# Two more places for expert weight pieces in an expert-choice MoE layer on one Trainium2 core

## What is computed

```python
def ec_moe(x, router_w, w1, w3, w2):
    probs = softmax(xf @ router_w)
    gates, idx = top_k(probs.T, cap)            # cap = 2 * N // 16: 64 and 16 rows
    xe = xf[idx]
    h = silu(xe @ w1) * (xe @ w3)               # per expert 1024 x 2048, twice
    ye = (h @ w2) * gates                       # per expert 2048 x 1024
    out = zeros_like(xf).at[idx].add(ye)

x = x + gate1 * (concat([o, s]) @ w_out)
h2 = rmsnorm(x, norm2_w) * (1 + scale2) + shift2
x = x + gate2 * ec_moe(h2, router_w, w1, w3, w2)
y = rmsnorm(x, final_norm_w)
```

## Time and profile before

| | |
|---|---|
| time, median of 3 runs (lowest, highest) | 1450.53 us (1450.44, 1455.31) |
| the profiled execution: its own time, its span | 1455.17 us, 1453.3 us |
| PE busy, share of the span | 1391.0 us, 96% |
| DVE, ACT, POOL busy | 356.9, 163.7, 56.0 us |
| HBM read, written | 455.67 MB, 13.37 MB |
| the loop of experts 1 to 14 | 489.3 to 1368.9 us |

### The profile page before, as it was taken

The page is one execution under the profiler, slowest core; times in us unless marked ns, Lnnn a source line. Parts: engine busy times, 40 slices in busy tenths (PEclk is TensorE's granted clock), DMA queues, the critical chain, the costliest instruction groups (busy, mean ns, idle before and its releaser), DMA issues.

```text
span 1453.3 us, 24452 instructions
## 1 busy us (share of the span) xinstructions
PE 1391.0 (96%) x10960; PEld 511.1 (35%) x10960; DVE 356.9 (25%) x709; ACT 163.7 (11%) x263; POOL 56.0 (4%) x65
## 2 busy tenths in 40 slices
PE   5899999899879999999999999999999999999994
PEld 2354544755533232323333333332323333232321
DVE  3116153523632111303111130211203111130314
ACT  3263324111120000000000000000000000000011
POOL 0200000000000000000000000000000000000000
PEclk8999999799989999999999999999999999999997
DMA  9433313401656999999999999999999999999995
GB/s 358 160 118 115 107 51 109 154 30 58 263 222 279 396 409 413 411 417 400 426 402 412 414 412 417 401 412 414 410 417 402 425 399 412 414 410 417 414 411 213
DMA packets 73357, 469.56 MB, mean 323 GB/s; under 512 B 4749, under 2 KB 6626, under 8 KB 32362
## 3 DMA queue, kind: packets, MB, share of 16 engines
q1 hardware_dynamic: 67200, 451.36, 76.3%
q0 software_dynamic: 5200, 17.17, 4.2%
q10 hardware_dynamic: 922, 0.52, 0.1%
HBM read 455.67 MB, written 13.37 MB: 323 GB/s over the span
## 4 chain that ended last, share of the span: by engine, by line
PE 85%; DMA 11%; DVE 2%; issue 1%; SPq 1%; ACT 1%; POOLq 0%; ACTq 0%; POOL 0%; DVEq 0%
PE psum L1016 41%; PE psum L1032 12%; PE psum L663 9%; DMA ring<-in_exp_w_dram 9%; PE psum L1043 6%; PE psum L876 5%; PE psum L707 2%; PE psum L644 1%; DMA ring<-in_ada_w_dram 1%; PE psum L967 1%; PE psum L901 1%; PE psum L850 1%; SPq L546 1%; PE psum L854 1%; DMA both<-xn_dram,both 1%
## 5 line engine op out<-in xcount | busy, mean ns | idle before, releaser
L1016 PE MATMUL psum<-ring,both 128*32 128x512 f32 x6144 | 665.4, 593 | 1.9 <-DMA ring<-in_exp_w_dram 0.8
L1016 PEld LDWEIGHTS psum<-ring,both 128*32 128x32 f32 x6144 | 198.0, 110 | 462.7 <-issue 434.7
L1032 PE MATMUL psum<-ring,both 128*32 128x512 f32 x2048 | 233.6, 597 | 6.3 <-DMA ring<-in_exp_w_dram 5.8
L1745 DVE TENSOR_TENSOR both<-both,psum 128x512 f32<-128x512 f32 x48 | 49.5, 1032 | 555.4 <-PE psum L1016 555.4
L663 PE MATMUL psum<-ring,feat 128*128 128x512 f32 x320 | 138.3, 593 | 0.0
L1321 ACT ACTIVATE both<-psum 128x512 f32<-128x512 f32 x48 | 28.7, 597 | 952.1 <-PE psum L1016 887.1
L1032 PEld LDWEIGHTS psum<-ring,both 128*32 128x32 f32 x2048 | 65.2, 110 | 154.0 <-issue 143.8
L1043 PE MATMUL psum<-ring,both 128*32 128x512 f32 x1024 | 118.7, 592 | 0.0
L663 PEld LDWEIGHTS psum<-ring,feat 128*128 128x128 f32 x320 | 60.5, 190 | 76.4 <-issue 76.3
L1763 DVE SCALAR_TENSOR_TENSOR both<-psum,both 64x512 f32<-64x512 f32 x32 | 24.0, 749 | 224.2 <-PE psum L1043 224.0
L876 PE MATMUL psum<-ring,both 128*128 128x512 f32 x160 | 73.9, 618 | 0.0
(11 more groups left out here) (221 smaller groups left out, 604.6 us busy)
## 6 DMA issues: line engine op xcount, KB each, us to landing
ring<-in_exp_w_dram SPq DMA_DIRECT2D x192, 2048.0 KB, 25.0
ring<-in_ada_w_dram SPq DMA_DIRECT2D x12, 2048.0 KB, 12.5
ring<-in_w_in_dram SPq DMA_DIRECT2D x4, 2048.0 KB, 12.8
ring<-in_w_out_dram SPq DMA_DIRECT2D x2, 2048.0 KB, 10.6
acc_dram<-x POOLq DMA_DIRECT2D x5, 512.0 KB, 2.9
xn_dram<-feat POOLq DMA_DIRECT2D x5, 512.0 KB, 2.9
x<-acc_dram SPq DMA_DIRECT2D x5, 512.0 KB, 26.5
out_dram<-feat SPq DMA_DIRECT2D x5, 512.0 KB, 10.4
```

What stands on the lines that cost most here:

```text
L1016: mm = nc.tensor.matmul(role_bank(role)[f4 * PART:(f4 + 1) * PART, :], xe[:, kt, part * PART:(part + 1) * PART], w[:, kt % 2, f4 * 512:(f4 ...
L1032: mm = nc.tensor.matmul(role_bank("Y_A")[at:at + PART, :], h[:, c, part * PART:(part + 1) * PART], w[:, f, half * 512:(half + 1) * 512], s ...
L1745: role_stored(nc.vector.tensor_tensor(h_rows[:, part, :].rearrange("p (c a) -> p a c", a=PART), silu_h[:, part % 2, :].rearrange("p (a c) ...
```

## The change

The four sample tiles of x, and those in `feat`, are each just the size of a piece. Both buffers become places for expert pieces: `IN_X` and `IN_FEAT`, so there are eight. Pieces are counted through all experts (n = 12 x expert + m) and go to place `EXPERT_SLOT[n % 8]`. Twelve isn't a multiple of eight, but 24 is, so the loops of SP and PE now take two experts in a body, and `piece_place` gives place and count for both; the loops of ACT and DVE stay as they are. A piece is loaded when the piece eight before it has been read.

Pieces 0 and 1 of expert 0 go to the new places and are the first that SP issues: piece 0 when the four sample tiles of x are saved and normed, piece 1 when the normed rows are saved and PE has turned them. The wait for the attention's last output comes then, ahead of piece 2. The load of the gate piece now stands ahead of piece 5 and behind pieces 0 to 4. At the end, the loads of x move from ahead of piece 9 to behind piece 11 and wait until PE has read piece 5 of the last expert. POOL waits for the saves of x ahead of its first gather.

```diff
-EXPERT_SLOT = [3, 4, 5, 2, 0, 1]
-LOADS_BEFORE = [CHUNK_SLOT.count(s) for s in range(RING)]
+IN_X, IN_FEAT = RING, RING + 1
+EXPERT_SLOT = [IN_X, IN_FEAT, 3, 4, 5, 2, 0, 1]
+PIECES = len(EXPERT_SLOT)
+LOADS_BEFORE = [CHUNK_SLOT.count(s) for s in range(PIECES)]
 EXPERT_LOADS = 12
+
+
+def piece_place(m, expert, ahead):
+
+    odd = not isinstance(expert, int)
+    n = EXPERT_LOADS * ((1 if odd else expert) + ahead) + m
+    slot = EXPERT_SLOT[n % PIECES]
+    loads = 16 * (LOADS_BEFORE[slot] + n // PIECES + 1)
+    per_expert = 16 * EXPERT_LOADS // PIECES
+    return slot, loads - per_expert + expert * per_expert if odd else loads
+
...
-        x = sb("x", TILES * D)[:].rearrange("p (t d) -> p t d", t=TILES)
+        x_all = sb("x", TILES * D)
...
         def chunk(slot):
+            if slot == IN_X:
+                return x_all[:, 0:CHUNK_F]
+            if slot == IN_FEAT:
+                return feat[:, 0:CHUNK_F]
             return ring[:, slot * CHUNK_F:(slot + 1) * CHUNK_F]
...
-        def wait_expert_chunk(pe, m, expert):
-            slot = EXPERT_SLOT[m % RING]
-            pe.wait_ge(slot_loaded[slot], 16 * (LOADS_BEFORE[slot] + m // RING + 1) + expert * (16 * EXPERT_LOADS // RING))
+        def wait_expert_chunk(pe, m, expert, ahead):
+            slot, loads = piece_place(m, expert, ahead)
+            pe.wait_ge(slot_loaded[slot], loads)
             return chunk(slot)
...
-        def wait_expert_chunk_read(sp, m, expert):
+        def wait_expert_chunk_read(sp, m, expert, ahead):
 
             back, m = (1, m + EXPERT_LOADS) if m < 0 else (0, m)
-            when = expert - back
+            when = expert + (ahead - back) if ahead != back else expert
...
-            def load_expert_chunk(m, expert):
-                slot = EXPERT_SLOT[m % RING]
+            def load_expert_chunk(m, expert, ahead=0):
+                slot, loads = piece_place(m, expert, ahead)
+                expert = expert + ahead if ahead else expert
...
 
 
-            wait_filled(sp, JOB["o", TILES - 1])
-            sp.wait_ge(o_ready, TILES)
-            for m in range(RING):
-                if m == 3:
+            for m in range(PIECES):
+                slot = EXPERT_SLOT[m]
+                if slot == IN_X:
+                    sp.wait_ge(acc_saved, 16 * ST)
+                    sp.wait_ge(xn2_ready, ST)
+                elif slot == IN_FEAT:
+                    sp.wait_ge(xn2_saved, 16 * ST)
+                    wait_filled(sp, JOB["hT", ST - 1, 0])
+                    wait_filled(sp, JOB["hT", ST - 1, 1])
+                elif slot == 3:
+                    wait_filled(sp, JOB["o", TILES - 1])
+                    sp.wait_ge(o_ready, TILES)
+                elif slot == 2:
                     wait_trunk_chunk_read(sp, CHUNK_OF["out", 0])
                     sp.dma_start(chunk(CHUNK_SLOT[CHUNK_OF[ADA[11]]]).rearrange("p (k n) -> p k n", k=KT), ada_k[:, :, 5632:6144])\
                         .then_inc(slot_loaded[CHUNK_SLOT[CHUNK_OF[ADA[11]]]], 16)
-                if m >= 3:
-                    wait_trunk_chunk_read(sp, chunk_before(EXPERT_SLOT[m], len(TRUNK_CHUNKS)))
+                if slot < TRUNK_RING:
+                    wait_trunk_chunk_read(sp, chunk_before(slot, len(TRUNK_CHUNKS)))
                 load_expert_chunk(m, 0)
-            for m in range(RING, EXPERT_LOADS):
-                wait_expert_chunk_read(sp, m - RING, 0)
+            for m in range(PIECES, EXPERT_LOADS):
+                wait_expert_chunk_read(sp, m - PIECES, 0, 0)
                 load_expert_chunk(m, 0)
-            with sp.Fori(1, LAST) as expert:
-                for m in range(EXPERT_LOADS):
-                    wait_expert_chunk_read(sp, m - RING, expert)
-                    load_expert_chunk(m, expert)
+            with sp.Fori(1, LAST, 2) as expert:
+                for ahead in range(2):
+                    for m in range(EXPERT_LOADS):
+                        wait_expert_chunk_read(sp, m - PIECES, expert, ahead)
+                        load_expert_chunk(m, expert, ahead)
             for m in range(EXPERT_LOADS):
-                if m == 9:
-                    sp.wait_ge(acc_saved, 16 * (TILES + LAST))
-                    for t in OUT_ORDER:
-                        sp.dma_start(x[:, t, :], acc_dram[t * P:(t + 1) * P, :]).then_inc(acc_loaded[t], 16)
-                wait_expert_chunk_read(sp, m - RING, LAST)
+                wait_expert_chunk_read(sp, m - PIECES, LAST, 0)
                 load_expert_chunk(m, LAST)
+            sp.wait_ge(w13_read, 6 * EXPERTS)
+            sp.wait_ge(acc_saved, 16 * (TILES + LAST))
+            for t in OUT_ORDER:
+                sp.dma_start(x[:, t, :], acc_dram[t * P:(t + 1) * P, :]).then_inc(acc_loaded[t], 16)
...
             pool.wait_ge(xn2_saved, 16 * ST)
+            pool.wait_ge(acc_saved, 16 * ST)
...
-            def expert_products(expert, first=False, last=False):
+            def expert_products(base, ahead=0, first=False, last=False):
+                expert = base + ahead if ahead else base
...
             expert_products(0, first=True)
-            with pe.Fori(1, LAST) as expert:
-                expert_products(expert)
+            with pe.Fori(1, LAST, 2) as expert:
+                for ahead in range(2):
+                    expert_products(expert, ahead)
```

More of the change, by code:

```diff
@@ L208, in trunk_kernel @@
         router_amp = sb("router_amp", 2 * KT * EXPERTS)[:].rearrange("p (w k e) -> p w k e", w=2, e=EXPERTS)
-        x = sb("x", TILES * D)[:].rearrange("p (t d) -> p t d", t=TILES)
+        x_all = sb("x", TILES * D)
+        x = x_all[:].rearrange("p (t d) -> p t d", t=TILES)
         feat = sb("feat", TILES * D)
@@ L292, in trunk_kernel @@
         psum_stored = [sem(f"psum_stored{b}") for b in range(BANKS)]
-        slot_loaded = [sem(f"slot_loaded{s}") for s in range(RING)]
+        slot_loaded = [sem(f"slot_loaded{s}") for s in range(PIECES)]
         extra_loaded = {name: sem(f"extra_loaded_{name}") for name in EXTRA}
@@ L1022, in up_chunk @@
                 def up_chunk(which, k2):
-                    return wait_expert_chunk(pe, EXPERT_CHUNKS.index((which, k2)), expert).rearrange("p (k n) -> p k n", k=2)
+                    return wait_expert_chunk(pe, EXPERT_CHUNKS.index((which, k2)), base, ahead).rearrange("p (k n) -> p k n", k=2)
                 def down_sample(i, w):
@@ L1047, in down_chunk @@
                 def down_chunk(i):
-                    return wait_expert_chunk(pe, 8 + i, expert).rearrange("p (k n) -> p k n", k=4)
+                    return wait_expert_chunk(pe, 8 + i, base, ahead).rearrange("p (k n) -> p k n", k=4)
                 if first:
```

## The result

The changed kernel takes 1515.95 us in the median of four runs (1510.72 to 1518.85), the kernel before 1450.49 beside it: ratio 1.0446, 95% interval 1.0414 to 1.0477. Forecast were 1449.7 us and a range up to 1470.5, so the time lies 66 us above the forecast and 45 above the range. It is rival B's direction: B had 19.6 us more than before, measured are 65.5. The profiled execution took 1510.72 us, its span 1508.9.

A forecast was written before the change was run, and what follows sets the result against it. PE and weight transfers were taken as level in the loop, the end as hanging on transfers. Gate weights 4.5 us later, stalls gone, jumps covered: x's scaling sets the end, 1450.5 - 0.8 = 1449.7 us, range 1444.5 to 1470.5.

The forecast's parts named there:

- rival B: PE's loop: body not held, each jump back stops PE for two packets; 25.8 us in all, 1470.1 us; chance 0.32.
- Part 4: PE's loop body of two experts: jumps back cost 0 to 3.6 us in all, under cover of 5.4 us.
- part 3: Tail, x loads behind last pieces: the 4.64 us wait goes, the end hangs on x; span 0.8 us less.
- The upper bound in the text: PE's jumps back: all 5.3 us of load on one packet, 5.2 us per jump plus 1.7 low clock, 41 in all.
- Held or not: PE's loop: whether a body of 9.4 code packets stays on the engine, where one of 4.7 does; no row shows it.
- Part 1: Before the first expert: five pieces ahead of the gate weights make them 4.5 us later (3.0 to 5.9), without slack.
- Part 2: Expert loop: a lead of two pieces, 10.0 us, removes stalls of 1.19 and 2.6 us, and lasts.
- Rival D: Expert loop: the two places bring no lead because SP stops at a full queue; span 1452.5, as forecast; chance 0.08.
- rival C: Before the first expert: the gate weights aren't held up; span 1448.0, time 1445.2 us; chance 0.14.

The follow-up runs named there:

- experiment 7: Kernel before with PE's two-expert loop body, six places, and the loop's weight loads cut to a sixteenth of their bytes; branch 3.8 us, a jump costs 7.0 us.
- experiment 3: Changed kernel with six transposes repeated in the first expert, shifting the loop's start by twelve instructions over a packet border; 1481.83 us, ratio 1.0201.
- experiment 1: Changed kernel with PE's fourteen middle experts written out one behind the other, no jumps back on PE; 1461.18 us, ratio 1.0063 to the kernel before.
- experiment 5: Kernel before with eight places, each piece always in the same place, PE's one-expert body, x loaded behind the last piece; 1445.35 us, ratio 0.9973.
- experiment 4: Kernel before with only the five loads of x moved behind the last weight piece; 1457.7 us, ratio 1.0034.

## Why the prediction was wrong

**Part 4 failed, in the price of a fetch.** The step was "2.7 us, 0.6 us of PE per jump, 3.6 in all", which part 3's 5.4 us were to cover; the jumps cost 11.4 us each, 68.4 in all. I had built 2.7 us from the landing of a 16 KB load on a quiet queue and 0.7 us for load. The branch took 6.1 us, 3.8 of them on quiet queues. A loaded queue adds 2.3, not 0.7, and behind the packet's end some 1.4 us pass until the branch ends (in experiment 7 too), which a landing row doesn't hold. The cover was right: 2.1 us of lead ahead of the jump against 6.1 leaves 4.0, and the first gaps are 3.9. The second term was the number of packets. For the forecast I took one; the loop's start stands ahead of a border, and it is two. Moving it (experiment 3) halves the gaps. The third was what a gap leaves behind it: 3.8 us per jump, some 2.7 of it at the lower clock, where rival B had 1.7 and the forecast none.

**B had the mechanism and the wrong size.** 2.6 + 1.7 = 4.3 us per jump was B's price, 7.6 + 3.8 = 11.4 measured, 68.4 against 25.8 in all. B's second fetch was priced at 2.0 us because it would follow the first directly. It doesn't: it begins only 3.2 to 3.7 us after the jump has ended, when the first packet is at work and PE's lead is gone, and it costs 3.55 us of idle time of its own. The upper bound in the text, 5.2 and 1.7 of clock per jump for one packet, was near experiment 3's 6.05. Carried to two packets and to the range's end it is 2 x 5.2 + 1.7 = 12.1 per jump, 73 in all, above the 68.4 measured; I had left it out of the range.

**Held or not.** I took "no row shows whether that stays" as nearly even. The Trainium skill (Runtime: NRT & Kernel Launch, section Instruction fetch mechanics) gives room for 2048 instructions, filled as a FIFO in blocks of 256. The body has 2,370 by the trace, and 103 packets agree with the Trainium skill; so does a body of 1,442 that stays. Bodies of 1,986 and 1,794 are not foretold by its 2048, as they are shorter and fetched again; there the measurement decides. The same section of the Trainium skill has a remark on a window of two pages. It does not hold for TensorE here: bodies of 1,187 and 1,442 instructions repeat without a packet. By the Trainium skill's 2048 alone rival B should have been the likeliest case.

**Part 1 was right, slightly high.** From the issue of the gate weights to PE's use of them 15.3 us passed (384.78 to 400.08), 11.8 before: 3.5 later, with 4.5 forecast and 3.0 as the lower bound. PE's wait grew by the same 3.5, to 6.6 (7.6 forecast). 2.7 of it reached the first expert, and the wait for the gathered rows stayed at 5.5: 0.8 us of slack in that line, where I had none.

**Part 2 was right in its mechanism.** No wait for weights is left in the kernel after; experiment 1 runs ten experts of 62.64. That the lead lasts came near for a body that is held (experiment 5: 1.0 us of waits, the last six experts at the pace of the transfers) and was wrong for straight code, which uses it up after ten experts.

**Part 3 had the mechanism right, and can't be read in the kernel after.** Only where PE is on time does the scaling run directly into the prompt rows: experiments 1, 4 and 5 show it with no idle time. The claim that the end then hangs on x is borne out by experiment 4's 4.9 us. Its size holds in experiment 5, whose order of pieces is another: the scaling starts 1002.5 us after the first expert, forecast were 1003.7. In experiment 1 it is 1014.2, as the supply is slower there, and the last expert's start to the end takes 88.7 us against 84.4 before: the places bring that kernel nothing.

**Rival D** is out by experiment 1, **rival C** by part 1's 3.5 us.

## What to carry to other kernels

Before a loop body grows, count its instructions on every engine and look at the code queue's packets inside the loop: none means that the body is held. Here a body too long was fetched again whole, for 11 us per jump. If buffers and work don't divide evenly, give some pieces a fixed place of their own rather than let the map rotate over a longer body; that turned a loss of 4.5% into a gain of 0.3% here (ratio 0.9973). And a lead was worth no more here than the waits that it covers, a few us in a kernel whose transfers and matmuls are level.

## What the runs showed of the hardware

- A body of 1,442 instructions stays on TensorE, one of 1,794 is fetched again whole, nine packets a pass. Neither loses only a part; lengths between the two were not run.
- A taken jump to code that isn't held occupies the sequencer for 5.9 to 6.2 us in the kernel after, whose DMA share is near 1, and for 3.6 to 3.9 us at 0.15. The packet itself takes 1.1 us in the first and 0.9 to 1.4 us in the second.
- Twelve instructions decide between one and two packets per jump, which is 34 us in this kernel (1481.83 against 1515.95).
- Two gaps of under 4 us with three matmuls between them bring the granted clock to 0.50 until 13.5 us after the first gap began (611.6 to 625.1). What a jump costs beyond its idle time is half as much again, 3.8 us on 7.6, and some 2.7 of that are the lower level.
- Straight code doesn't stop PE, but in the only kernel here that ran it the weights arrived 1.1% more slowly (63.55 us per expert against 62.83), with 4.6 code packets per expert on the same engines (cause inferred).
